# Opening of the gated layers: the row squares are added up on GpSimd instead of VectorE, and the matmul that counts them moves into the third panel

## The reference, cut to what matters

```python
def rmsnorm(x, g):
    xf = x.astype(jnp.float32)
    y = xf * lax.rsqrt(jnp.mean(xf * xf, axis=-1, keepdims=True) + RMS_EPS)
    return (y * g.astype(jnp.float32)).astype(x.dtype)

def swiglu(h, w_gate, w_up, w_down):
    return (jax.nn.silu(h @ w_gate) * (h @ w_up)) @ w_down

def second_block(x, norm_g, ...):            # x is 1 x 512 x 1024
    h = x
    for layer in range(2):
        ...                                  # m: attention, or the pooling mixer
        h = h + rmsnorm(m, g[1])
        u = rmsnorm(h, g[2])
        h = h + rmsnorm(swiglu(u, ffn_w_gate[layer], ffn_w_up[layer], ffn_w_down[layer]), g[3])
    return h
```

## Time and profile before

| | us |
|---|---|
| runs of the kernel before | 1890.84, 1893.62 (median), 1895.72 |
| the profiled execution's own time | 1894.11 |
| its span in the profile | 1892.3 |
| TensorE matmul busy | 1806.5 (95% of the span) |
| VectorE busy | 1269.2 (67%) |
| ScalarE busy | 944.6 (50%) |
| GpSimd busy | 311.0 (16%) |
| mean granted TensorE clock | 0.987 |

### The profile page before, as it was taken

How to read it: one execution, slowest core, us unless ns; L and a number is a source line. 1 busy time by engine, 2 the same in 40 slices (tenths; PEclk the granted TensorE clock), 3 DMA queues, 4 the chain that set the end, 5 groups by cost and what they waited for, 6 DMA issues and landing times. The chain is left out here.

```text
span 1892.3 us, 37560 instructions
## 1 busy us (share of the span) xinstructions
PE 1806.5 (95%) x15453; PEld 1570.6 (83%) x15453; DVE 1269.2 (67%) x1991; ACT 944.6 (50%) x1659; POOL 311.0 (16%) x355
## 2 busy tenths in 40 slices
PE   7999989889999999999998899999999899999998
PEld 6777777758999888777976688999998788999997
DVE  4346667547767676666367748677777777777776
ACT  6633444435644444345348647544444674544444
POOL 4012656524200000000023203000005030000000
PEclk9999999999999999999979999999999999999999
DMA  5222000002223323273100122333333112333332
GB/s 189 90 67 87 6 3 4 12 24 89 90 92 109 112 90 112 73 137 99 57 1 1 36 77 71 98 108 106 107 107 121 45 57 67 101 102 104 106 105 76
DMA packets 152238, 148.30 MB, mean 78 GB/s; under 512 B 13676, under 2 KB 150026, under 8 KB 152074
## 3 DMA queue, kind: packets, MB, share of 16 engines
q1 hardware_dynamic: 151948, 145.91, 25.0%
q10 hardware_dynamic: 126, 0.04, 0.0%
HBM read 143.84 MB, written 2.10 MB: 77 GB/s over the span
## 5 line engine op out<-in xcount | busy, mean ns | idle before, releaser
L1725 DVE TENSOR_TENSOR weight_low<-weight_ring,weight_high 128x1024 fp32r<-128x1024 f32 (+2 forms) x250 | 254.2, 1022 | 147.0 <-ACT weight_high L1713 146.8
L1713 ACT CAST weight_high<-weight_ring 128x1024 fp32r<-128x1024 f32 (+2 forms) x250 | 215.2, 864 | 249.3 <-PE psum L247 121.0
L1760 PE MATMUL psum<-tail_x_high,weight_high 128*128 128x256 f32 x1008 | 283.6, 281 | 5.1 <-ACT tail_quads L1832 5.1
L1762 PE MATMUL psum<-tail_x_high,weight_low 128*128 128x256 f32 x1008 | 283.2, 281 | 0.0
L1761 PE MATMUL psum<-tail_x_low,weight_high 128*128 128x256 f32 x1008 | 283.1, 281 | 0.0
L1760 PEld LDWEIGHTS psum<-tail_x_high,weight_high 128*128 128x128 f32 x1008 | 190.6, 189 | 7.7 <-issue 3.3
L1761 PEld LDWEIGHTS psum<-tail_x_low,weight_high 128*128 128x128 f32 x1008 | 190.5, 189 | 1.6
L1762 PEld LDWEIGHTS psum<-tail_x_high,weight_low 128*128 128x128 f32 x1008 | 190.5, 189 | 0.0
L245 PE MATMUL psum<-tail_hidden_high,weight_high 128*128 128x512 f32 (+1 forms) x480 | 176.7, 368 | 2.5 <-DVE tail_hidden_low L4385 2.5
L247 PE MATMUL psum<-tail_hidden_high,weight_low 128*128 128x512 f32 (+1 forms) x480 | 176.1, 367 | 0.0
L246 PE MATMUL psum<-tail_hidden_low,weight_high 128*128 128x512 f32 (+1 forms) x480 | 176.0, 367 | 0.0
(11 more groups left out here) (530 smaller groups left out, 4573.2 us busy)
## 6 DMA issues: line engine op xcount, KB each, us to landing
weight_ring<-in_w_ff SPq DMA_DIRECT2D x32, 1024.0 KB, 5.4
weight_ring<-in_ffn_w_gate SPq DMA_DIRECT2D x22, 1024.0 KB, 5.4
weight_ring<-in_ffn_w_up SPq DMA_DIRECT2D x22, 1024.0 KB, 5.4
weight_ring<-in_ffn_w_down SPq DMA_DIRECT2D x32, 512.0 KB, 4.6
weight_ring<-in_rw_in SPq DMA_DIRECT2D x11, 1024.0 KB, 5.2
weight_ring<-in_attn_w_in SPq DMA_DIRECT2D x9, 1024.0 KB, 5.3
weight_ring<-in_ffn_w_down SPq DMA_DIRECT2D x8, 768.0 KB, 4.4
weight_ring<-in_w_out SPq DMA_DIRECT2D x4, 1024.0 KB, 4.9
```

The source lines that it names most:

```text
L1713: last = act.copy(high, source)
L1725: last = dve.tensor_tensor(low, source, high, ALU.subtract)
L1760: pe.matmul(out, w_hi, x_hi, start=kk == 0 and not more, stop=False, skip_group_check=more)
L1762: last = pe.matmul(out, w_lo, x_hi, start=False, stop=kk == kp - 1, skip_group_check=more)
```

## The change

The seven additions leave `open_dve` and become `add_rows` on GpSimd, ahead of the four turns; the wait for `before.counted` that guards the memory of `total` goes with them. The count leaves the second token half of position 1, where it stood after the fifth of eight blocks, and stands in position 2 after the fourth of eight blocks. ScalarE's stream is unchanged, its waits for `x_added` and `x_counted` included.

```diff
@@ open_pe
-                    elif pos == 1 and kt == KT // 2:
-                        pe.wait_ge(self.x_added, KT - 1)
-                        pe.matmul(k.ps[:, 6, :], k.ones[:], t.total[:], start=True, stop=True).then_inc(self.x_counted, 1)
         for pos in range(2, GATED_OPEN):
...
                 if kt == KT // 2 - 1:
                     last.then_inc(stream.halved, 1)
+                    if pos == 2:
+                        pe.wait_ge(self.x_added, KT - 1)
+                        pe.matmul(k.ps[:, 6, :], k.ones[:], t.total[:], start=True, stop=True).then_inc(self.x_counted, 1)
@@ open_dve
-        dve.wait_ge(before.counted, len(PARTS))
-        for b in range(1, KT):
-            dve.wait_ge(self.x_squared, b + 1)
-            if b > 1:
-                dve.wait_ge(self.x_added, b - 1)
-            dve.tensor_tensor(t.total[:], t.row_squares[:, 0, :] if b == 1 else t.total[:], t.row_squares[:, b, :], ALU.add).then_inc(self.x_added, 1)
@@
+    def add_rows(self, pool, before):
+        t = self.t
+        pool.wait_ge(before.counted, len(PARTS))
+        for b in range(1, KT):
+            pool.wait_ge(self.x_squared, b + 1)
+            if b > 1:
+                pool.wait_ge(self.x_added, b - 1)
+            pool.tensor_tensor(t.total[:], t.row_squares[:, 0, :] if b == 1 else t.total[:], t.row_squares[:, b, :], ALU.add).then_inc(self.x_added, 1)
+
+    def pool(self, pool, before):
+        self.add_rows(pool, before)
         for q in range(KT // 2):
             self.differences.turn(pool, q)
```

More of the change, by code:

```diff
@@ L4014, in add @@
         self.add_squares(dve, 10)
-    def pool(self, pool):
+    def add_rows(self, pool, before):
[8 more added lines that the diff above has]
+        self.add_rows(pool, before)
         for q in range(KT // 2):
@@ L4042, in _ @@
         def _(pool):
-            self.pool(pool)
+            self.pool(pool, before)
 POOL_WINDOWS = (2, 4, 8, 16)
```

## The result

The changed kernel takes **1904.68 us** in the median of 4 executions (1903.30 to 1906.21), against 1892.23 us for 4 of the kernel before (1889.99 to 1895.72). The ratio is 1.0063, with a 95% interval of 1.0050 to 1.0077: 9.5 to 14.6 us slower. The forecast was 1905, slower by 11.2 us. Later runs brought the executions of the kernel before to 27, with a median of 1891.77 us; against that the changed kernel is 12.9 us slower.

What follows compares the result with a forecast made beforehand. The prediction took each layer's opening to be bound by the ScalarE, VectorE and GpSimd chain from logarithm to second copy. Delays of 7.4 and 5.4 us, less 1.6 us of clock loss, gave 11.2 us: 1905 us, range 1901.5 to 1911.

Steps and rivals of the forecast that it cites:

- What bounds the opening: Position 4's PSUM copy in both layers: the ScalarE, VectorE and GpSimd chain sets it, about 28.9 us behind the logarithm.
- The additions: Before the root: seven GpSimd additions take 11.3 us, ending about 1155.2 and 1551.1; VectorE's freed 5.4 us per layer gain nothing.
- The count: In position 2 behind 24 matmuls: starts at 1158.9 and 1552.5, making the logarithm 7.6 and 5.4 us later.
- The shift: From root to second copy in position 4: the copy comes 7.4 and 5.4 us later, together 12.8 us.
- The shortening kept for the range: GpSimd's later pair 0 turns might shorten the chain before pair 2: 0.5 us per layer, not counted in the forecast.
- The clock: Half clock at position 4's start in both layers, hidden behind the chain; none behind the copy, so 1.6 us goes away.
- The sum: Whole kernel: 12.8 us lost less 1.6 us gives 11.2 us slower, 1905 us.
- old clock loss: Behind the second layer's 2.1 us stop in position 4: 18 matmuls at mostly 1.2 GHz, 1.6 us lost, expected to go.
- rival 1: At the count in position 2: all seven additions collide and TensorE waits, 3.9 us more, 1909 us; chance 0.13.
- ScalarE's own order doesn't hold it up: Before the logarithm: after the seventh addition, two gained copies (1.34 us) and a cast (some 1 us) end by 1157.7.
- rival 2: VectorE's load, not the root, sets the opening's end; 5.4 us per layer saved, 1882.6 us; chance 0.02.
- rival 3: Early turns of pairs 0 and 1: GpSimd sets the chain before pair 2, absorbing the delay; 1894.5 us, chance 0.06.

Runs made afterwards that it cites:

- count alone: Kernel before with only the count moved to position 2, the seven additions still on VectorE: 1903.72 us, ratio 1.0053 to the kernel before.
- count earlier: Changed kernel with the count two blocks earlier in position 2, behind 12 matmuls instead of 24: 1903.34 us, ratio 1.0059 to the kernel before.
- count later: Changed kernel with the count at the end of position 2, behind 48 matmuls instead of 24: 1916.01 us, ratio 1.0120 to the kernel before.
- additions alone: Changed kernel with the count back in position 1, the seven additions still on GpSimd: 1907.17 us, ratio 1.0066 to the kernel before.

## Why the prediction was right

**What bounds the opening** held. The second copy follows the logarithm by 28.4 to 29.1 us in both layers of five kernels with the order of before (before, changed, count alone, count earlier, count later), while the logarithm itself moves between 9.5 and 22.6 us. The exception, 30.7 and 30.8 us, is the kernel in which TensorE was made later than the chain.

Two readings behind this were less exact than they looked, without harm to the forecast. The prediction takes the agreement of 29.08 and 28.88 us as the sign of a chain that runs on its own durations. In the second layer of the kernel before it does. In the first, TensorE held it by a little: the cast of position 4's last weights, ahead of the join, waited 0.34 us for the end of position 3, where the same cast had no wait in the second layer (it is the second of the two in its row):

```profile
1176.86 1.05 ACT L1713 CAST weight_high<-weight_ring 128x1024 fp32r<-128x1024 f32 x1 [0.34 <-PE psum L247]
...
1571.78 1.56 ACT L1713 CAST weight_high<-weight_ring 128x512 fp32r<-128x512 f32 x2
```

That the two distances agreed to 0.2 us was in part luck. In the changed kernel TensorE stands still for 5 us ahead of this place, so nothing of it is left.

And it wasn't the count alone that set the logarithm of the kernel before. It starts 9.5 us behind the first square in both layers, although the count starts at 8.4 in one and 6.8 in the other. In the first layer the count and ScalarE are ready together. In the second the logarithm comes 1.6 us behind the count's end, right behind ScalarE's gained copies and a weight cast:

```profile
1544.75 2.56 ACT L3482 ACTIVATE tail_pairs<-residual_T,columns_b 128x512 f32<-128x512 f32 x4
1547.21 1.04 ACT L1713 CAST weight_high<-weight_ring 128x1024 fp32r<-128x1024 f32 x1
```

So the floor that the run with the earlier count met at 15.0 us stood at 9.5 us before the change.

**The additions.** Forecast: five steps at 1.35 us and two at 2.25, ended at 1155.2. Measured: 1144.05 to 1155.58, with two collisions. (A free step took 1.44 us, 0.09 more than forecast, a collided one 2.25.) Costed at nothing on VectorE: right, it now idles instead.

**The count.** Forecast at 1158.9 and, counted from the square, 13.8; measured 1160.00 and 13.8. The 1.1 us of the first layer come from before the first moved instruction: in the profiled execution the clock was at half for 3.4 us in the first token half, and TensorE came through there with 13 matmuls,

```profile
1134.20:1137.60 3.40, 2.94 (x13) 2.94 (x14) 3.33 (x8) 0.91 (x2) 0.00 (x0) 0.50 0.54 170
```

where the kernel before made 24 in the same stretch. Matched matmul by matmul that is a loss of 1.3 us; none of the other eight traces has this stretch. The kernels with the count in the same place and no such stretch have it at 15.9 and 16.2 us behind the first square, where the forecast's 1158.9 is 16.1.

**The shift.** Forecast +7.4 and +5.4 us to the copy. Measured, from the first square, +8.3 and +5.7; the 8.3 less the 1.1 to 1.3 just named is 7.0 to 7.2, so 12.6 to 12.8 in all (the count alone, without that stretch, has +7.0 in the first layer). The shortening kept for the range was 0.6 us in the first layer and none in the second. In the first, VectorE's low part of pair 0 ran at 1.22 us instead of 1.76, Silu held pair 2 (1166.28 + 1.06, gained copies at 1167.24), and TensorE's 0.34 us were gone. In the second the root came before GpSimd was through with its late turns: the low part of pair 0 took 1.76 us again, and ScalarE waited for it before pair 2:

```profile
1565.60 1.34 ACT L3482 ACTIVATE tail_pairs<-residual_T,columns_b 128x512 f32<-128x512 f32 x2 [0.41 <-DVE tail_x_low L3500]
```

The count alone, with turns at the old time, has 28.5 us there against 29.0: here the late turns cost 0.5 us, where the prediction has them cost nothing.

**The clock.** Forecast: half clock behind the first stop, hidden, and none behind the copy. Stretches of the changed kernel of the kind of the earlier trace rows, from position 4 on in the first layer, then from the stop on in the second:

```profile
1182.50:1189.00 6.50, 6.11 (x29) 6.14 (x30) 5.05 (x7) 4.75 (x7) 0.00 (x0) 0.52 0.08 8
1190.00:1196.00 6.00, 5.95 (x50) 5.97 (x50) 4.75 (x8) 0.99 (x2) 0.00 (x0) 1.00 0.62 208
1577.90:1581.20 3.30, 0.00 (x0) 0.00 (x0) 3.30 (x6) 0.86 (x2) 0.00 (x0) 0.50 0.00 0
1581.00:1586.00 5.00, 4.76 (x27) 4.79 (x28) 3.98 (x6) 4.35 (x6) 0.00 (x0) 0.63 0.00 0
...
1588.40:1594.00 5.60, 5.59 (x47) 5.60 (x48) 4.37 (x7) 0.76 (x2) 0.00 (x0) 1.00 0.67 227
```

The fourth product starts at 2.4 GHz in both layers, and the old loss behind the second layer's copy is gone. But the clock fell while TensorE still stood, 3.3 us before the end of the stop in the second layer and 0.9 us in the first. So the 1.2 GHz level covers 28 of the 36 matmuls in the first layer and 16 in the second, not all of them. It is hidden in both: position 4 to fourth product takes 7.2 us either way. In the first layer this is close: the fourth product follows the third without a stop to speak of (0.2 us more than a slot), where the second has 1.1 us. With all 36 at the half clock the 7.4 us of the prediction would have come out a little behind the chain.

**The sum.** 11.2 us forecast, 11.9 us by the ratio (9.5 to 14.6). The profiled executions differ by 9.2 us. Matched matmul by matmul, the changed one loses 8.3 us in the first opening (1.3 of it the stretch at 1134) and 4.0 in the second, and gains 2.9 us between 1499 and 1517, where the kernel before ran through two stretches of half clock that the changed kernel's execution did not have; what is left is 0.2 us. Without the stretches outside the chain the two openings cost 11.0 us. One term rests on traces alone: the 1.6 us taken off for the old clock loss. It is seen in one execution of each kernel, and the times can't settle it, because the interval holds 12.8 us as well as 11.2.

**The rivals.** A late seventh addition (rival 1) did not occur with the count in position 2, but the second layer had 1.0 us left where I had put 1.4, and the runs with an earlier count show it at work. One point of mine was wrong there without harm: "ScalarE's own order doesn't hold it up". In the second layer it does, by 0.2 us: gained copies and cast end with the count, and the logarithm starts 1.24 us behind the count's start instead of 1.07. VectorE's load (rival 2) would have shown without a stop in position 4. The shift taken up (rival 3) would have left 0.4 us of the 12; it is refuted by the distance of 28.5 to 29.0 us and by the later count, where 5.6 us per layer came out as 11.3 us in the time.

## What to carry to other kernels

A sum that leaves the busiest vector engine is worth nothing if it stands in front of a short serial step (here count, logarithm, root) on which everything behind waits: follow that step's result to the next place where the bound engine waits, and if a wait is there already, nearly every microsecond by which the step moves comes back in the time. Two layers of the same code with TensorE standing differently against the chain are a cheap sign of what sets the end: if the distance from a landmark to the wait is the same in both, the chain is probably bound by itself. It is no proof: here the two distances agreed to 0.2 us though TensorE held one of them, and in the run with the additions alone they agreed to 0.1 us because TensorE held both. Read each engine's waits along the chain as well, for one that ends with TensorE. And an order written by hand should be read for waits that stand in front of something urgent; here ScalarE's wait for the seventh addition, ahead of pair 1, sets a floor under the root that rises with the additions.

## What was not expected of the hardware

Half-clock stretches of 3.4 us appear in some executions and not in others, in places where the kernel is the same. One lies at 1134 us in the changed kernel's profile. Two lie at 1499 and 1513 us in that of the kernel before; of the other eight traces five have one or two in that part, and three have none. Each cost 1.2 to 1.7 us. Most of the scatter between executions goes with the clock: the eight executions of the kernel before with a mean granted clock of 0.991 or 0.992 took 1887.9 to 1890.3 us, the five with 0.986 or 0.987 took 1893.7 to 1897.0. So single profiled executions of this kernel are comparable to some 3 us only, and what a change does to one stage is read more sharply from a landmark inside the stage than from the span.

The longest stretches near the openings go with stops, and begin inside them. In the run with the additions alone, the 6.5 us stop of the second layer goes with about 10 us of half clock, of which more than 4 us lie in the stop. Behind it TensorE came through with 19 matmuls in the 5.4 us that were left of the window shown (granted clock 0.50). The stops of 5.0 and 5.7 us in the changed kernel go with 7 us of it, of which 0.9 and 3.3 us lie in the stop and cost nothing. The stop of 2.1 us in the kernel before was followed by 3.7 us at a granted clock of 0.55. None of the stops of 0.8 us for the copy, in four kernels, was followed by any half clock.
